# Output product of two FFN layers: six of twelve weight-block sums moved from VectorE to accumulating DMAs issued by GpSimd

## The reference, cut to what matters

```
def swiglu(x, w1, w3, w2):
    return (jax.nn.silu(x @ w1) * (x @ w3)) @ w2      # x 512x1024, w1/w3 1024x2816, w2 2816x1024

for layer in range(2):
    ...
    h = layer_norm(alpha * h + mix, ...)
    ffn = swiglu(h, ffn_w1[layer], ffn_w3[layer], ffn_w2[layer])
    h = layer_norm(alpha * h + ffn, ...)
```

## Time and profile before

| | us |
|---|---|
| median of three runs | 1157.22 (1156.43 to 1158.26) |
| the profiled execution | 1156.23 |
| its span, first to last instruction | 1154.5 |
| PE busy in the span | 1133.9 (98%) |
| DVE, ACT, POOL busy | 863.0 (75%), 541.4 (47%), 525.2 (45%) |
| DMA traffic | 121.00 MB, mean 105 GB/s |
| output product, layer 0 | PE's first matmul at 449.5 |
| output product, layer 1 | PE's first matmul at 1035.5 |

### The profile page before, as it was taken

The page is one execution under the profiler, slowest core; times in us unless marked ns, Lnnn a source line. Parts: engine busy times, 40 slices in busy tenths (PEclk is TensorE's granted clock), DMA queues, the critical chain, the costliest instruction groups (busy, mean ns, idle before and its releaser), DMA issues.

```text
span 1154.5 us, 19191 instructions
## 1 busy us (share of the span) xinstructions
PE 1133.9 (98%) x7461; PEld 988.1 (86%) x7461; DVE 863.0 (75%) x1202; ACT 541.4 (47%) x849; POOL 525.2 (45%) x346
## 2 busy tenths in 40 slices
PE   7999999999999999999999999999999999999997
PEld 6877768899999999888887777777999999998886
DVE  8558652897888888994804787866987888879957
ACT  6335665245444544553335555532545454454540
POOL 6897614356567773010353232203576666760000
PEclk9999999999999999999999999999999999999999
DMA  7623315143333336234243111202433333352341
GB/s 213 186 76 93 109 65 201 39 126 110 110 100 103 108 105 192 72 113 143 86 133 91 56 56 55 67 8 74 130 89 111 110 105 97 100 179 88 96 123 73
DMA packets 160186, 121.00 MB, mean 105 GB/s; under 512 B 19376, under 2 KB 140248, under 8 KB 160096
## 3 DMA queue, kind: packets, MB, share of 16 engines
q1 hardware_dynamic: 160096, 119.77, 34.7%
HBM read 116.32 MB, written 3.43 MB: 104 GB/s over the span
## 4 chain that ended last, share of the span: by engine, by line
PE 92%; DVE 5%; ACT 1%; POOL 1%; issue 1%; SPq 0%; DMA 0%; DVEq 0%; ACTq 0%; POOLq 0%
PE ps L2122 18%; PE ps L2124 17%; PE ps L2123 17%; PE ps L2154 5%; PE ps L2152 5%; PE ps L2153 5%; PE ps L2145 5%; PE ps L2147 5%; PE ps L2146 5%; PE ps L2661 2%; PE ps L2687 2%; PE ps L2672 2%; PE ps L2159 1%; PE ps L2705 1%; PE ps L2384 1%; PE ps L2707 1%
## 5 line engine op out<-in xcount | busy, mean ns | idle before, releaser
L848 POOL TENSOR_TENSOR wlo<-raw,whi 128x1024 fp32r<-128x1024 f32 x75 | 183.2, 2454 | 333.4 <-ACT whi L973 326.4
L2122 PE MATMUL ps<-xhi,whi 128*128 128x256 f32 (+1 forms) x848 | 272.1, 321 | 0.0
L2124 PE MATMUL ps<-xhi,wlo 128*128 128x256 f32 (+1 forms) x848 | 267.0, 315 | 0.0
L2123 PE MATMUL ps<-xlo,whi 128*128 128x256 f32 (+1 forms) x848 | 266.9, 315 | 0.0
L2122 PEld LDWEIGHTS ps<-xhi,whi 128*128 128x128 f32 x848 | 161.7, 191 | 17.6 <-issue 6.4
L927 POOL TENSOR_TENSOR wlo<-raw,whi 128x512 fp32r<-128x512 f32 x114 | 173.2, 1546 | 0.6 <-ACT whi L1235 0.4
L2124 PE MATMUL ps<-thi,wlo 128*128 128x256 f32 x608 | 172.2, 283 | 0.0
L2123 PE MATMUL ps<-tlo,whi 128*128 128x256 f32 x608 | 172.2, 283 | 0.0
L2122 PE MATMUL ps<-thi,whi 128*128 128x256 f32 x608 | 172.2, 283 | 0.0
L2124 PEld LDWEIGHTS ps<-xhi,wlo 128*128 128x128 f32 x848 | 161.8, 191 | 10.4
L2123 PEld LDWEIGHTS ps<-xlo,whi 128*128 128x128 f32 x848 | 161.9, 191 | 8.5
(11 more groups left out here) (293 smaller groups left out, 2355.6 us busy)
## 6 DMA issues: line engine op xcount, KB each, us to landing
raw<-in_ffn_w SPq DMA_DIRECT2D x126, 512.0 KB, 3.9
raw<-in_odd_w_in SPq DMA_DIRECT2D x24, 512.0 KB, 3.7
raw<-in_even_w_in SPq DMA_DIRECT2D x16, 512.0 KB, 4.5
t<-in_ffn_w SPq DMA_DIRECT2D x12, 512.0 KB, 6.4
h<-in_x SPq DMA_DIRECT2D x8, 512.0 KB, 5.0
raw<-in_even_w_out SPq DMA_DIRECT2D x8, 512.0 KB, 3.8
raw<-in_odd_w_out SPq DMA_DIRECT2D x8, 512.0 KB, 3.5
bias<-rel_scratch SPq DMA_DIRECT2D x8, 256.0 KB, 3.5
```

The lines of the kernel that those rows point to most:

```text
L848: eng.tensor_tensor(lo, raw_of(b), hi, ALU.subtract).then_inc(w_lo, 1)
L2122: eng.matmul(o_, w_hi_, x_hi_, start=start, stop=False)
L2123: eng.matmul(o_, w_hi_, x_lo_, start=False, stop=False)
L2124: return eng.matmul(o_, w_lo_, x_hi_, start=False, stop=stop)
```

## The change

The sums `3t` and `1t` of all three batches, six of the twelve of a layer, leave DVE. In their place POOL issues two DMAs for each batch (`add_left`), which read U right and U left from w2 in HBM and add them to what stands in `t3` and `t1` (the right halves that SP loaded). They wait until both of SP's loads of the batch have landed (`t_landed[b]`). Batch 0's pair stands between `plain_lowers` and the lo tiles of the first three units, batches 1 and 2 behind these. Who read the two sums now waits for semaphores of these DMAs, `t3_summed[b]` and `t1_summed[b]`: ACT's `out_upper` for P5 and P7, and DVE's `2t`. The slot of a `1b` unit is reloaded when `2t` alone is done. The other tables change only in that the six names drop out.

```
+            def add_left(layer, b):
+                pool.wait_ge(t_landed[b], 32 * (layer + 1))
+                for store, column, added in ((t3, S, t3_summed), (t1, 0, t1_summed)):
+                    eng.dma_start(store[:, 2 * b:2 * b + 2, :], tiles_of(w2[layer], 2 * b * P, column, S, 2),
+                                  accum_op=ALU.add).then_inc(added[b], 16)
 ...
                 split[0] = out_first(layer)
-                lower_upto(out_first(layer) + FIRST_UNITS)
+                for b in range(BATCHES):
+                    add_left(layer, b)
+                    if b == 0:
+                        lower_upto(out_first(layer) + FIRST_UNITS)
 ...
-                    if name == "3t":
-                        dve.wait_ge(t_landed[b], 32 * (layer + 1))
-                        tt(pair_sum(P7, b), pair_sum(P7, b), pair_sum(P5, b), ALU.add).then_inc(t_sum, 1)
-                    if name == "1t":
-                        tt(pair_sum(P5, b), pair_sum(P5, b), upper, ALU.add).then_inc(t_sum, 1)
-                    if name == "2t":
+                    if name == "2t":
                         dve.wait_ge(*landed(out_block(layer, P1, b)))
                         dve.wait_ge(half_used, products_upto(layer, SEVENS - 1, P3))
-                        dve.wait_ge(t_sum, t_sum_upto(layer, f"3t{b}"))
+                        dve.wait_ge(t3_summed[b], 16 * (layer + 1))
                         tt(pair_sum(P6, b), pair_sum(P7, b), upper, ALU.add).then_inc(t_sum, 1)
 ...
-EARLY_SUMS, FIRST_SUMS = "1s0 1s1", "3t0 1t0 2t0"
+EARLY_SUMS, FIRST_SUMS = "1s0 1s1", "2t0"
 SUMS_BEHIND = (
-    {2: "3s0 3s1", 3: "3t1", 4: "1t1 2t1", 5: "N0 3t2 2t2", 8: "N1 1s2", 9: "3s2 N2", 10: "1t2", 12: "4t0", 16: "4t1",
+    {2: "3s0 3s1", 4: "2t1", 5: "N0 2t2", 8: "N1 1s2", 9: "3s2 N2", 12: "4t0", 16: "4t1",
```

More of the change, by code:

```diff
@@ L141, in build @@
     GS = 7 * BATCHES
-    SUMS = ("3t", "1t", "2t", "4t"), ("1s", "3s", "N", "L")
+    SUMS = ("2t", "4t"), ("1s", "3s", "N", "L")
     def ffn_blocks(layer):
@@ L226, in t_sum_upto @@
     def t_sum_upto(layer, name):
-        return 4 * BATCHES * layer + sums_listed(layer, SUMS[0]).index(name) + 1
+        return 2 * BATCHES * layer + sums_listed(layer, SUMS[0]).index(name) + 1
     def g_sum_upto(layer, name):
@@ L476, in build @@
         t_landed = [sem(f"t_landed{b}") for b in range(BATCHES)]
+        t1_summed, t3_summed = ([sem(f"{name}_summed{b}") for b in range(BATCHES)] for name in ("t1", "t3"))
         x_sum, t_hi, t_lo = sem("x_sum"), sem("t_hi"), sem("t_lo")
@@ L660, in weights_upto @@
                                 if kind == P1:
-                                    sp_.wait_ge(t_sum, max(t_sum_upto(layer, f"{n}t{part}") for n in (1, 2)))
+                                    sp_.wait_ge(t_sum, t_sum_upto(layer, f"2t{part}"))
                                 if kind in (P2, P4):
@@ L1275, in out_upper @@
                     b_ = out_first(layer) + u
-                    if kind in (P5, P6, P7, P4):
-                        act.wait_ge(t_sum, t_sum_upto(layer, {P5: "1t", P6: "2t", P7: "3t", P4: "4t"}[kind] + str(part)))
+                    if kind in (P5, P7):
+                        act.wait_ge((t1_summed if kind == P5 else t3_summed)[part], 16 * (layer + 1))
+                    elif kind in (P6, P4):
+                        act.wait_ge(t_sum, t_sum_upto(layer, {P6: "2t", P4: "4t"}[kind] + str(part)))
                     else:
@@ L1955, in t_sums @@
                     upper = raw[:, raw_slot(out_block(layer, P1, b)), :].rearrange("p (k n) -> p k n", k=2)
-                    if name in ("1t", "2t"):
+                    if name == "2t":
                         dve.wait_ge(*landed(out_block(layer, P1, b)))
-                    if name == "3t":
-                        dve.wait_ge(t_landed[b], 32 * (layer + 1))
-                        tt(pair_sum(P7, b), pair_sum(P7, b), pair_sum(P5, b), ALU.add).then_inc(t_sum, 1)
-                    if name == "1t":
-                        tt(pair_sum(P5, b), pair_sum(P5, b), upper, ALU.add).then_inc(t_sum, 1)
-                    if name == "2t":
                         dve.wait_ge(half_used, products_upto(layer, SEVENS - 1, P3))
-                        dve.wait_ge(t_sum, t_sum_upto(layer, f"3t{b}"))
+                        dve.wait_ge(t3_summed[b], 16 * (layer + 1))
                         tt(pair_sum(P6, b), pair_sum(P7, b), upper, ALU.add).then_inc(t_sum, 1)
```

## The result

| | before | after |
|---|---|---|
| median, us | 1156.83 (1156.43 to 1158.26) | 1183.49 (1180.71 to 1187.24) |
| ratio, 95% interval | | 1.0229 (1.0201 to 1.0256) |
| profiled execution, its span | 1156.23, 1154.5 | 1185.75, 1184.0 |
| mean granted clock in the span | 0.998 | 0.991 |
| DMA traffic, MB | 121.00 | 127.29 |

The change makes the kernel slower: it costs 26.7 us in the medians and 29.5 in the profiled executions. The page of the changed kernel first: busy time (against the earlier trace rows), the DMA queue that POOL's DMAs go through (packets, MB, share of 16 engines' span), and the DMA issues with their median time to landing.

The account below looks back on a forecast made before the run. PE's order of matmuls alone was taken to bound the kernel, so no gain; waits of 9.8 us in layer 0 and 4.6 in layer 1, 14.4 together, gave 1172 us after the median's 1.0 and rounding, range 1162 to 1200.

Parts of the forecast that it names:

- a slow add: Rival: each accumulate holds the DMA engines 8 us, delaying 5b0 and 6b1; 1188 to 1215 us, chance 0.15.
- gain of DVE's 13.6 us: Six sums a layer leave DVE, 13.6 us in all, beside matmuls that never wait for it: gain 0.
- layer 0, before A0: PE waits 3.6 us for POOL's first lo tile, held behind SP's two loads and two DMA issues.
- before 1b2, before 5b0: Layer 0: PE waits 1.2 and 5.0 us for DVE's lo tiles queued behind sums 2t1 and 2t2.
- layer 1, before A0: PE waits 2.2 us for POOL's first lo tile, held behind SP's two loads and two DMA issues.
- before 2b0, before 2b1: Layer 1: PE waits 2.4 us before 2b0 for lo tiles behind 2t1; no wait was forecast before 2b1.
- half clock: PE's clock falling in three waits, 4 us of half clock each: 6 us more, 1178, left out of the sum.
- The sums on DVE: Layer 0: batch 0's first accumulate lands at 454.5 and 2t0 ends on DVE at 455.7.
- The accumulate: Each accumulating DMA takes 2.8 us of all 16 engines plus 2.0 us latency, landing after 4.8 us.
- that of place alone: Rival: only POOL's place costs, accumulates land as fast as loads, DVE's sums stay hidden; 1161 to 1163 us, chance 0.17.
- the issue of 3.8 us: Rival: an issue on POOL costs near 3.8 us, first waits 17 us together; 1180 to 1184 us, chance 0.09.
- that it is no slower: Rival: batch 0 lands early enough that PE does not wait for A0; 1157 us or less, chance 0.09.

Follow-up runs that it names:

- e9: Changed kernel with accumulating DMAs for batches 1 and 2 alone, POOL's lo tiles first, 2t1 and 2t2 later in DVE's order: 1156.85 us, 0.9994.
- e10: Like e9, but accumulating DMAs for batch 2 alone (two a layer), 2t2 of layer 0 behind unit 8: 1158.80 us, 1.0010.
- e12: Changed kernel with 36 identity transposes on PE before unit A0 in both layers, into an unread PSUM bank: 1180.24 us, 1.0195.
- e3: Kernel before, with POOL waiting for batch 0's pair of SP loads ahead of its three lo tiles, no POOL DMA: 1163.34 us, 1.0053.
- e1: Changed kernel with POOL's three lo tiles ahead of all its accumulating DMAs: 1170.22 us, 1.0110.
- e6: e5 with 2t0 as well behind the fourth unit's lo tile on DVE: 1163.47 us, 1.0052.
- e4: Changed kernel with POOL's DMAs as plain copies, without the add: 1168.78 us, 1.0097.
- e7: e1 with plain copies in place of the accumulating DMAs: 1165.06 us, 1.0063.
- e5: e1 with 2t1 and 2t2 later in DVE's order: 1165.60 us, 1.0068.
- e8: e1 with batch 0's two sums back on DVE, accumulating DMAs for batches 1 and 2 alone: 1165.36 us, 1.0066.
- e11: e10 with 2t2 of layer 0 in its old place behind unit 5: 1162.34 us, 1.0040.

## Why the prediction was right or wrong

The direction and the mechanism held: no gain, a wait at A0 ended by POOL's lo tile, and later waits ended by DVE's lo tiles behind sums that wait for DMAs. The other signs that were named came too: ACT's first wait for a load stays short (0.5 us, 0.4 before), and 6.3 MB more are moved. The time lay 11.5 us above the forecast of 1172, inside the range. That the range held is in part luck: it reached up to 1200 for the sake of a slow add, which did not come, and not for what did. (Its price for that rival has a slip: twice 31 us gives 1219 and not 1215.) By steps:

| step | forecast | trace |
|---|---|---|
| gain of DVE's 13.6 us | 0 | 0 (e9, e10, with eight and four of the twelve sums moved) |
| layer 0, before A0 | 3.6 | 4.9 |
| before 1b2, before 5b0 | 1.2, 5.0 | 1.4, 2.2 |
| layer 1, before A0 | 2.2 | 6.6 |
| before 2b0, before 2b1 | 2.4, 0 | 1.0, 3.8 |
| sum of waits | 14.4 | 19.9 |
| half clock | 0 in the sum, 6 "on top" | 7.6 |

**The clock** is the largest miss. It was priced at 6 us and left out of the sum, on the ground that the clock was 1.00 in all stretches but the last. That row could not speak of waits of 4 to 7 us, since PE had none. Priced in, the forecast would have been 1178. e12 shows that the fall comes from PE's idleness: the same wait with PE busy has none.

**The wait before A0.** From the landing to A0's first matmul it took 5.3 us in layer 0 and 5.2 in layer 1, where I had 4.4. The lo tile took its 2.4; the pair of issues took 2.6 in layer 0 and 2.4 in layer 1 for the 2.0 said, and POOL started 0.3 behind the landing. In layer 0 the pair landed 7.2 us after the first issue, with 6.9 forecast. In layer 1 it took 9.1, and SP issued 7.7 us ahead of PE's turn and not 9.1. The earlier trace rows give 5.6 to 8.5 with the median 6.4; a sum for a wait that counts from its last microsecond should have taken the spread, 2.1 us, into it. e3 gave this step alone: 5.8 us over, which is the forecast of the two waits by coincidence: it is made of 2.9 us of gaps before A0, a fall of the clock and what came behind.

**The sums on DVE.** `2t0` was to end at 455.7 and began at 462.76. The DMA alone was not the cause (it landed at 457.2, 5.7 after issue; 4.8 was said). DVE was held by POOL's subtractions, which the forecast had moved beside it without asking what the two do to each other. e3 shows the collision without any DMA, e1 its end when the subtractions go first. Of its price I know only that DVE got to `2t0` 5.6 us after the landing.

**The slot behind `2t1`.** For layer 1 I followed the sum to 2b0 and not to the load of 2b1, which needs the slot that `2t1` reads:

```profile
1076.66 0.37 SPq L672 DMA_DIRECT2D raw<-in_ffn_w  x1
```

```profile
1085.36 1.04 ACT L1293 CAST whi<-raw 128x1024 fp32r<-128x1024 f32 x1 [13.90 <-DMA raw<-in_ffn_w]
```

`2t1` ends at 1076.6, SP issues at once, and the load lands 8.7 us later behind the accumulates. I had used this rule for 1b2 and stopped there. e6 shows the same thing in layer 0.

**The accumulate.** 2.8 us of the engines were said, 3.06 measured, but by two errors that cancel: a copy on the same queue takes 1.46 and not 1.9, and the add makes it 2.1 times as long and not one and a half times. The landing was off: 4.8 us said, 8.8 in the median, since the engines had up to four other loads in work. The Trainium skill, Collectives: The Full Stack, The bandwidth ceiling, has the add halve the rate by its two source reads. The ratio measured here, 3.06 to 1.46, is 2.1 and agrees. The estimate of 3.8 us that the prediction made by that page was too high, since it doubled the 1.9.

**5b0 cost less** than said (2.2), since PE arrived late itself, by 1.3 us of longer wait and 1.7 of half clock at A0 besides the late start, while the DMA for it (483.3) was only as late as forecast, with the 2.1 of the late start.

Of the rivals, that of place alone (1161 to 1163) is refuted by the changed kernel, and even with the add taken out it is not met (e4, 11.2 over). The slow add of 8 us and the issue of 3.8 us are refuted by their rows; that it is no slower, by the gaps and the time. What stays open is how the 15 us of the add in place divide between its engine time and its longer issue: 2.0 us before A0 are the issue, and for the rest no run changed the one without the other. Open too is why an operation of DVE got through between POOL's instructions in e3 and in the changed kernel only behind all three. The variation of 6.5 us among the four times of the changed kernel was not traced either.

## What to carry to other kernels

Work taken from an engine that nobody waits for gives nothing, and a sum that hangs on a second transfer behind the first is late by two landings: it needs a reader that stands far behind (e9, e10), and every slot that the reader frees counts as one of those who wait. Put a wait on an engine's queue only behind the work that others want from it. When a change opens gaps of 2 us or more, as here, on a TensorE that was full, put the half-clock time behind each gap into the sum, and when it moves GpSimd's arithmetic, look up which VectorE operations it will now stand beside.

## What the runs showed of the hardware

- A GpSimd-issued accumulating DMA of 512 KB from HBM into SBUF holds the 16 engines for 3.06 us, a copy of the same shape for 1.46. The engine's issue lasts 1.19 to 1.70 us against 0.72 to 0.89, a pair 2.57 against 1.61, and packets are 272 against 144 for each DMA.
- VectorE operations with both inputs in SBUF stand still beside GpSimd's subtractions: 9.12 us for two that take 1.28, 8.98 for one of 0.68; those with an operand in PSUM take 0.69 and 0.70 as ever (e3). The Trainium skill, SBUF — State Buffer, SBUF: two separate sides, says that the two engines share a port pair which the one that starts first holds for a whole instruction. The blocking agrees, and in e3 the length does: there one operation of VectorE got through behind each of POOL's instructions (3.90 for two, 2.87). But e4's 8.15 us and the 9.12 of the changed kernel reach over all three of POOL's instructions, so there the hold lasted for a back-to-back run of them and not for one. In e3 no DMA of POOL's stands ahead of the run, and the VectorE operation begins in the middle of it; which of these matters no run shows.
- The clock fell to 1.2 GHz in or right behind waits of PE of 4.9, 6.6, 2.2 and 3.8 us, for 3.41 or 6.83 us; the matmuls' step went from 0.23 to 0.43 us. Behind waits of 1.0 to 1.8 us (changed kernel, e3, e6, e7) it did not fall, behind those of 2.1 to 4.0 in e1, e3, e5, e7, e8, e11 and e12 it did. With transposes on PE in the wait at A0 (e12) it stayed at 2.4 GHz.
